# Sixteen narrow expert places instead of fourteen, in a period of five, in a hybrid attention and mixture-of-experts layer

## What is computed

```python
def moe(h, w_router, b_router, w_gu, b_gu, w_down, b_down):
    logits = hf @ w_router + b_router                  # 512 x 32
    top_vals, top_idx = lax.top_k(logits, 4)
    gates = jax.nn.softmax(top_vals, axis=-1)
    # every (token, expert) pair, grouped by expert:
    gu = xb @ w_gu[e] + b_gu[e]                        # 1024 -> 2048
    glu = jnp.minimum(gu[:, :1024], 7.0)
    lin = jnp.clip(gu[:, 1024:], -7.0, 7.0)
    act = glu * jax.nn.sigmoid(1.702 * glu) * (lin + 1.0)
    y = (act @ w_down[e] + b_down[e]) * g              # 1024 -> 1024
    out = segment_sum(y, token)                        # and x is added
```

## Time and profile before

| what | us |
|---|---|
| median of three runs (1442.34 to 1444.7) | 1443.8 |
| the profiled execution, its own time | 1444.39 |
| its span | 1442.6 |
| PE busy | 1346.2 |
| VectorE busy | 1257.3 |
| ScalarE busy | 1121.1 |
| GpSimd busy | 216.1 |

### The profile page before, as it was taken

How to read it: one execution, slowest core, us unless ns; L and a number is a source line. 1 busy time by engine, 2 the same in 40 slices (tenths; PEclk the granted TensorE clock), 3 DMA queues, 4 the chain that set the end, 5 groups by cost and what they waited for, 6 DMA issues and landing times. The chain is left out here.

```text
span 1442.6 us, 18459 instructions
## 1 busy us (share of the span) xinstructions
PE 1346.2 (93%) x6570; PEld 1086.7 (75%) x6570; DVE 1257.3 (87%) x1314; ACT 1121.1 (78%) x1227; POOL 216.1 (15%) x143
## 2 busy tenths in 40 slices
PE   6999878999999999998999899999899989998995
PEld 5887766776788877876787677777678767876784
DVE  4799778548899999999999899999999999998995
ACT  5666664455787998898888888888888988888874
POOL 1112000012111131111121011210111111210221
PEclk9999979999999999999999999999999999999998
DMA  5422111148999999999999999999999999999991
GB/s 152 146 74 59 45 59 45 44 165 305 332 384 367 378 415 407 382 402 395 393 392 395 398 391 381 396 399 386 396 382 388 390 387 390 388 392 386 399 398 53
DMA packets 85924, 448.50 MB, mean 311 GB/s; under 512 B 18496, under 2 KB 23616, under 8 KB 36608
## 3 DMA queue, kind: packets, MB, share of 16 engines
q1 hardware_dynamic: 73424, 428.32, 74.7%
q0 software_dynamic: 9792, 18.90, 5.4%
q10 hardware_dynamic: 2608, 0.01, 0.1%
HBM read 440.89 MB, written 23.07 MB: 322 GB/s over the span
## 5 line engine op out<-in xcount | busy, mean ns | idle before, releaser
L840 DVE TENSOR_TENSOR whl<-wraw,whl 128x2048 fp32r<-128x2048 f32 x384 | 863.3, 2287 | 69.9 <-ACT whl L835 68.4
L835 ACT ACTIVATE whl<-wraw 128x2048 fp32r<-128x2048 f32 x384 | 727.6, 1916 | 135.1 <-PE ps L2164 87.5
L2164 PE MATMUL ps<-whl,xT 128*128 128x512 f32 x2672 | 640.0, 394 | 11.6 <-DVE whl L840 9.8
L2164 PEld LDWEIGHTS ps<-whl,xT 128*128 128x128 f32 x2672 | 493.8, 188 | 128.2 <-DVE whl L840 17.1
L2164 PE MATMUL ps<-whl,aT 128*128 128x512 f32 x1264 | 304.0, 396 | 7.5 <-DVE whl L840 7.5
L2164 PEld LDWEIGHTS ps<-whl,aT 128*128 128x128 f32 x1264 | 236.4, 190 | 60.5 <-DVE whl L840 12.2
L1030 POOL DMA_INDIRECT out_dram<-ysb,idx x32 | 85.3, 2667 | 646.0 <-ACT ysb L1345 629.9
L1021 POOL DMA_INDIRECT xg<-h_rows,idx x32 | 83.5, 2611 | 230.4 <-DVE idx L1795 227.0
L1907 PE MATMUL ps<-W,HT 128*128 128x512 f32 (+1 forms) x184 | 73.1, 397 | 5.7 <-DVE W L612 4.7
L1909 PE MATMUL ps<-W,HT 128*128 128x512 f32 (+1 forms) x184 | 70.1, 381 | 0.0
L1908 PE MATMUL ps<-W,HT 128*128 128x512 f32 (+1 forms) x184 | 69.8, 379 | 0.0
(11 more groups left out here) (296 smaller groups left out, 1408.1 us busy)
## 6 DMA issues: line engine op xcount, KB each, us to landing
wraw<-in_w_gu_dram SPq DMA_DIRECT2D x256, 1024.0 KB, 15.8
wraw<-in_w_down_dram SPq DMA_DIRECT2D x128, 1024.0 KB, 13.5
WR<-in_w_in_dram SPq DMA_DIRECT2D x20, 512.0 KB, 3.6
WR<-in_w_o_dram SPq DMA_DIRECT2D x8, 512.0 KB, 3.9
xs<-in_x_dram SPq DMA_DIRECT2D x4, 512.0 KB, 7.7
WR<-in_x_dram SPq DMA_DIRECT2D x4, 512.0 KB, 3.5
out_dram<-WR SPq DMA_DIRECT2D x4, 512.0 KB, 2.6
h_rows<-WR SPq DMA_DIRECT2D x4, 512.0 KB, 2.6
```

What stands on the lines that cost most here:

```text
L835: act.activation(whl[:, n % HL, 0, :], wraw[n % RAW], ACT.Copy).then_inc(chunk_hi, 1)
L840: eng.tensor_tensor(whl[:, n % HL, 1, :], wraw[n % RAW], whl[:, n % HL, 0, :].bitcast(F32), ALU.subtract).then_inc(chunk_lo, 1)
L2164: ins = pe.matmul(bank, a[x_][j], w[:, b, j, 512 * q:512 * q + 512], start=c == NG and j == 0 and n == 0, stop=last and j == nj - 1 and n ...
```

## The change

The narrow places go from fourteen to sixteen and stand in a period of five from place 4 on: two narrow, one wide, one narrow, one wide. `WIDE` goes from 18 to 16, and the table `ordered` is filled to match: the narrow places take ranks 16 to 31 (places 4, 5 and 7 take 16, 17 and 18, the next three 19, 20 and 21, and so on, place 30 rank 31), the wide places ranks 4 to 15.

```diff
 FIXED = 4
-NARROW = sorted([4, 5, 8, 9, 12, 13, 16, 19, 20, 23, 24, 27, 28, 30])
+NARROW = sorted([5 * a + b for a in range(5) for b in (4, 5, 7)] + [30])
 WIDE = E - len(NARROW)
...
-            for j, n, first in ((4, 4, 18), (5, 3, 19), (19, 3, 25), (20, 3, 26), (30, 1, 31), (6, 3, 4), (7, 3, 5),
-                                (17, 4, 10), (18, 3, 11), (31, 1, 17)):
-                link(pool.iota(ordered[:, j:j + 4 * n - 3:4], pattern=[[2, n]], base=first, channel_multiplier=0,
+            for j, n, first, step in ((4, 5, WIDE, 3), (5, 5, WIDE + 1, 3), (7, 5, WIDE + 2, 3),
+                                      (6, 5, FIXED, 2), (8, 5, FIXED + 1, 2), (29, 1, WIDE - 2, 1), (30, 1, E - 1, 1), (31, 1, WIDE - 1, 1)):
+                link(pool.iota(ordered[:, j:j + 5 * n - 4:5], pattern=[[step, n]], base=first, channel_multiplier=0,
                                allow_small_or_imprecise_dtypes=True))
```

## The result

The changed kernel takes **2512.4 us** (median of 4 runs, 2511.0 to 2515.45); before takes 1443.59 us beside it (4 runs). The ratio is 1.7406, with a 95% interval of 1.7386 to 1.7427. The profiled execution took 2511.0 us with a span of 2509.2. The time was forecast at 2517 us, in a range of 2475 to 2590.

A forecast was written before the change was run, and what follows sets the result against it. Transfers were taken to bound the kernel, PE and VectorE close behind. One token too many forces a second round at PE's pace: 1444.4 - 3 + 1075.8 = 2517 us, range 2475 to 2590.

The forecast's parts named there:

- The case: Ranks 16 and 17 have 65 tokens for 64 slots; the tested value reaches 130, over 128, so a second round runs.
- first round, less than before: The first round gets 3 us shorter, between 0 and 10, as transfers hide most of PE's 9.4 us saving.
- restart: Start of the second round, from the last scatter through tables, index, gather and transposes to the first product: 10.7 us.
- place 0, with the cold clock: Second round, first product to the next bias product: 26.9 us as in the first round, plus 3 for the clock.
- 30 steps, with register waits: Second round, place 1 to place 31: 967 us at PE's pace plus 10 us for register instructions.
- place 31 to the last product: Second round, from place 31's bias product to the last product: 46.2 us, taken from the first round's times.
- end: Last rows and scatter of the second round, plus two skipped rounds with their branches: 12 us.
- 967 us of PE's steps: Thirty second-round steps priced by kind at 35.6, 30.4, 27.9 and 35.1 us, sum 967.3; ends 945 and 1010.
- The cold clock: PE idles before the second round, so place 0 starts at the 1.2 GHz level: 3 us added, between 0 and 10.
- Register waits: Register instructions working out semaphore values in PE's loop cost 10 us; exposed, 70 to 120 us more, chance 0.08.
- DMA share: Sign: the DMA engines' busy share stays 0.99 to 1.00 in the first round and falls below 0.97 in the second.
- the other signs: 768 rows of L840 and L835, PE at 96% or more, a 20 to 25 us PE gap with lowered clock, given step lengths.

The follow-up runs named there:

- E3: The kernel before with a fifteenth narrow place, 29, taking rank 17 with 65 tokens, and rank 16 in wide place 31: 2519.16 us in one run.
- E1: The changed kernel with narrow places counted once in the test for more rounds, so 65th tokens are left out and one round runs: 1443.76 us, ratio 1.0003.
- E2: The kernel before, fourteen narrow places, with ranks from 4 on counted twice in the test, so a second round runs and finds no token: 2521.42 us.
- E4: The kernel before with only half of each weight chunk loaded after the first eight chunks: 1416.37 us, ratio 0.9814.
- E5: The changed kernel held to one round, 65th tokens left out, with half of each weight chunk loaded after the first eight: 1407.40 us, ratio 0.9751.
- E9: The changed kernel, two rounds, with only half of each weight chunk loaded after the first eight chunks: 2470.01 us.
- E10: The changed kernel held to one round, with gathers and scatters moving at most row 0 and weights loaded in full: 1404.26 us, ratio 0.9732.

## Why the prediction was right

**The case.** The reading of the packets held. Rank 17 has 65 tokens, so sixteen narrow places overflow, `cnt` passes 128 and a second round runs. E3 shows that rank 17 alone does it, E1 that nothing else in the change costs time, and E2 that the round costs as much with no token in it.

**The terms**, as the prediction put them, and as measured in the profiled execution:

| term | forecast us | measured us | from |
|---|---|---|---|
| first round, less than before | 3 | 0 | last scatter landed by 1442.7, span of before 1442.6 |
| restart | 10.7 | 12.1 | 1454.78 - 1442.70 |
| place 0, with the cold clock | 29.9 | 26.6 | 1481.42 - 1454.78 |
| 30 steps, with register waits | 977 | 970.4 | 2451.84 - 1481.42 |
| place 31 to the last product | 46.2 | 45.1 | 2488.62 + 8.35 - 2451.84 |
| end | 12 | 12.2 | 2509.2 - 2497.0 |

The measured terms of the second round sum to 1066.4 us against 1075.8, and the whole is 2511.0 against 2517, an error of 0.2%.

The second round and its pace by PE were reasoned. That the sum comes within 0.2% is in part luck, because errors in it cancel. The largest pair lies in the 967 us of PE's steps. By their kinds, the steps of the second round measure:

| kind of step | count | forecast us | measured us |
|---|---|---|---|
| wide after wide | 4 | 142.4 | 145.0 |
| narrow after wide | 11 | 334.4 | 349.2 |
| narrow after narrow | 5 | 139.5 | 139.5 |
| wide after narrow | 10 | 351.0 | 336.8 |

The forecast took one step of each kind from the start of the first round. A narrow place after a wide one took 30.3 us only in place 4 and 29.8 in place 30, which have more than one wide place ahead of them, and 32.1 to 32.2 in the nine others; a wide one after a narrow one took 32.7 to 34.6. So the price also depends on the place before the last, and 15 us too little met 14 us too much. The 967.3 us were called an upper bound of PE's own work; 970.4 was measured with no transfer in the way.

**What was off.**
- *The first round's 3 us.* E1 leaves nothing of them: it is 0.1 us slower than before (ratio 1.0003, interval from 0.0006 faster to 0.0012 slower). E4 and E5 show why: the two narrow places take 10.1 us off PE, and what the transfers cost on top grows by 12. In the changed kernel something else came in at its end. SyncE starts to load the second round's first eight chunks while the last scatters are on their way: from 1424 to 1436 us the core moved 252 GB/s, before 23. ScalarE waited 12.05 us for place 30's scatter where it waited 7.85 before. That is a collision that the prediction did not name. The other runs bear it out: the wait is 11.9 us in E2 and E3, which also load on, 9.2 in E9 with half of each chunk, and 8.1 in E1, where nothing is loaded any more.
- *The restart.* It took 1.4 us longer than forecast, by two differences that go opposite ways. Up to the transposes it was shorter, 5.3 us (1442.70 to 1448.00) against 7.3 in the first round (337.42 to 344.71). From there to the first weight product it took 6.8 us against 3.0, because ScalarE splits the first chunks after the gathered rows in a later round (L835 at 1450.50), and before them in the first.
- *The cold clock.* The mechanism was right and its size was not: 3 us were put down for place 0. The granted clock was 0.91 over the 18.08 us from the first weight product to L2096, where the first round had 1.00, so about 1.6 us were lost there (an estimate, 0.09 of 18.08). E2 and E3, whose clock stayed at 0.50 until about 1460 us, some 5 us into place 0, took 27.3 us for place 0, the changed kernel 26.6. It lies below the forecast 29.9 for another reason as well: the first round's 26.9 us has products in it that the second round does not do (L2127 and L2150, 0.60 and 1.20 us ahead of L2096). Within the restart the transposes took 1.97 us where they took 1.06 in the first round; the bias product took 2.05, but PE waited 2.71 us for VectorE behind it, so that cost nothing.
- *Register waits.* The 10 us are not there, and the trace of after shows the instructions themselves, on the sequencer of PE's weight loads, here the two ahead of each chunk's products:

```profile
L2156 PEldq ALU_OP  x383: 32/32/32, 1454.8 to 2490.0; - x192
```

  Each took 32 ns, not the 260 ns of the gap at L2096. The idle time of PE's weight loads that is put down to issue is 21 us in these steps and 21 in E10's, which has none of them. The second round's steps, with them, sum to 970.4 us, and the first round's without them, in E5 and E10, where the transfers do not bind either, to 973.4. Of that difference 2.2 us lie in the step of place 1, where the first round has further products of its own; the other 29 steps sum to 932.8 us with the instructions and 933.6 without. The Trainium skill (Advanced Engine Details and Errata, Sequencer Loop) says that the sequencer executes a control instruction while engine instructions stay queued, and these runs agree. The gap ahead of L2096 is 7.1 us in 27 in both rounds. The branches that skip rounds 2 and 3 are in the trace too: L854 took 71 to 254 ns a time on PE, 39 to 69 on the other engines, within the under 1 us that was put down.
- *DMA share.* It was to fall below 0.97 in the second round and stayed at 0.97 to 0.98. The sentence on what sets the pace was right (E9), but its sign was badly chosen: a busy share near one does not tell a queue that others wait for from one that is only kept full. The waits for a landing do: 72 us in the first round, none in the second. Of the other signs, 768 rows, PE at 97% and the gap came: 25 us from the last product of one round to the first weight product of the next, with 5 us of small products in them and the clock at its lower level up to 3 us before its end. Of the step lengths 30.4 us did not come, as said above.

## What to carry to other kernels

A capacity that is checked on the chip makes the time a step function of the data: look for the branch, find the value that it tests, and read from the trace (packets of the last scatter, rows skipped) how near it is, before any engine time is added up. Here 64 slots met 65 tokens and one percent of engine time was set against 74% of the whole. And where two resources are both near 100% busy, who waits for whom tells which one binds; a test that halves one of them settles it.

## What the runs showed that was not expected

- A busy share of the DMA engines of 0.97 to 0.98, at 385 to 390 GB/s, is not a bound there: halving the bytes of that stretch changed its steps by 0.1 us in 970 (E9).
- The first round's steps have the same floor with half the weight bytes, 973.38 us, and with full weights but no rows, 973.37 us. The rows' 4% of the bytes are worth 38 us of 1011.
- A scatter or gather whose slots are all empty is not free for GpSimd: in the second round a scatter issue took 3557 ns on average, where it took 2852 in the first. A gather issue took less, 1976 ns against 2838. GpSimd's busy time went from 216 to 510 us in two rounds, 117 us of it in small writes (L1020 and L1029) that the first round does not have; in the steps it hid beside PE. Times on GpSimd are rough in the profile.
